# Thirteen products without a reader taken out between the router and the first gate product of a decoder block

## What is computed

```python
x = x + mix @ w_o[l]
h = rms_norm(x, norm_ffn_g[l]).reshape(b * s, d)
# moe_ffn, cut:
logits = (h @ w_router + b_router).astype(jnp.float32)
top_val, top_idx = lax.top_k(logits, TOP_K)
gates = jax.nn.softmax(top_val, axis=-1).astype(h.dtype)
# for every expert e, on the tokens that chose it:
g = xb @ w_gate[e] + b_gate[e]
u = xb @ w_up[e] + b_up[e]
g = jnp.minimum(g, SWIGLU_LIMIT)
u = jnp.clip(u, -SWIGLU_LIMIT, SWIGLU_LIMIT)
glu = g * jax.nn.sigmoid(SWIGLU_ALPHA * g)
out = ((u + 1.0) * glu) @ w_down[e] + b_down[e]
```

## Time and profile before

| | |
|---|---|
| median of 3 runs | 1124.85 us (1124.01 to 1125.22) |
| the profiled execution, its own time | 1124.24 us |
| its span in the trace | 1122.5 us, so 1.7 us lie around it |
| PE busy | 1066.8 us (95%) |
| DVE, ACT, POOL busy | 222.9, 126.1, 20.0 us |
| DMA traffic | 438.16 MB, 390 GB/s over the span |
| mean granted PE clock over the span | 0.988 of full speed |

### The profile page before, as it was taken

How to read it: one execution, slowest core, us unless ns; L and a number is a source line. 1 busy time by engine, 2 the same in 40 slices (tenths; PEclk the granted TensorE clock), 3 DMA queues, 4 the chain that set the end, 5 groups by cost and what they waited for, 6 DMA issues and landing times.

```text
span 1122.5 us, 11859 instructions
## 1 busy us (share of the span) xinstructions
PE 1066.8 (95%) x5057; PEld 504.1 (45%) x5057; DVE 222.9 (20%) x507; ACT 126.1 (11%) x226; POOL 20.0 (2%) x21
## 2 busy tenths in 40 slices
PE   9999999999999999999999898989898989999886
PEld 8888887634343443344334332433243324343322
DVE  5442223321112030203112110020203020202021
ACT  1201340210010001000100010000000100010002
POOL 2300000000000000000000000000000000000000
PEclk9999999999999999999999999999999999999999
DMA  8975256599999999999999999999999999999995
GB/s 339 391 307 225 85 216 281 197 403 429 434 431 431 429 431 430 433 430 433 432 433 431 430 433 431 433 430 433 433 432 431 430 433 431 433 426 426 429 427 241
DMA packets 26654, 438.16 MB, mean 390 GB/s; under 512 B 4992, under 2 KB 6272, under 8 KB 8576
## 3 DMA queue, kind: packets, MB, share of 16 engines
q1 hardware_dynamic: 26480, 437.67, 92.1%
q10 hardware_dynamic: 144, 0.07, 0.0%
HBM read 436.28 MB, written 1.05 MB: 390 GB/s over the span
## 4 chain that ended last, share of the span: by engine, by line
PE 58%; DMA 40%; ACT 1%; issue 0%; DVE 0%; another core or an unknown queue 0%; SPq 0%; ACTq 0%; DVEq 0%
DMA ring<-in_experts 40%; PE ps L1593 24%; PE ps L1639 9%; PE ps L1226 9%; PE ps L1402 2%; PE ps L1241 2%; PE ps L1507 2%; PE ps L1648 2%; PE ps L1276 1%; PE ps L1450 1%; PE ps L1447 1%; PE ps L1628 1%; PE ps L1516 1%; ACT region_va L708 0%; PE ps L1526 0%; DMA ring<-in_first 0%
## 5 line engine op out<-in xcount | busy, mean ns | idle before, releaser
L1593 PE MATMUL ps<-ring,xT 128*64 128x512 f32 x2048 | 462.8, 607 | 24.1 <-DMA ring<-in_experts 24.1
L1593 PEld LDWEIGHTS ps<-ring,xT 128*64 128x64 f32 x2048 | 145.0, 139 | 315.8 <-issue 283.6
L1639 PE MATMUL ps<-ring,region_va 128*64 128x512 f32 x1024 | 228.3, 596 | 22.9 <-ACT region_va L708 12.3
L1639 PEld LDWEIGHTS ps<-ring,region_va 128*64 128x64 f32 x1024 | 73.3, 137 | 156.4 <-issue 125.8
L1226 PE MATMUL ps<-ring 128*128 128x256 f32 x448 | 98.7, 380 | 0.0
L1226 PEld LDWEIGHTS ps<-ring 128*128 128x128 f32 x448 | 84.5, 190 | 11.8 <-issue 0.2
L1125 DVE TENSOR_SCALAR g<-ps 128x1024 f32<-128x1024 f32 x16 | 19.6, 1224 | 348.5 <-PE ps L1593 348.5
L1507 PEld LDWEIGHTS ps<-sel,x 128*128 128x128 f32 x480 | 55.4, 192 | 9.5 <-issue 9.5
L1648 PE MATMUL ps<-g,g_T 128*128 128x512 f32 x128 | 59.2, 605 | 0.0
L1147 DVE TENSOR_SCALAR region_va<-ps 128x512 f32<-128x512 f32 x32 | 22.1, 691 | 184.4 <-PE ps L1593 184.4
L1072 DVE TENSOR_TENSOR xT<-ps,g_ffn 128x512 f32<-128x512 f32 x30 | 20.7, 691 | 190.9 <-PE ps L1507 190.9
(11 more groups left out here) (218 smaller groups left out, 476.8 us busy)
## 6 DMA issues: line engine op xcount, KB each, us to landing
ring<-in_experts SPq DMA_DIRECT2D x71, 4096.0 KB, 46.2
ring<-in_experts SPq DMA_DIRECT2D x43, 2048.0 KB, 46.2
ring<-in_head SPq DMA_DIRECT2D x13, 2048.0 KB, 13.3
ring<-in_experts SPq DMA_DIRECT2D x14, 1024.0 KB, 8.5
ring<-in_first SPq DMA_DIRECT2D x7, 384.0 KB, 6.4
x<-in_x SPq DMA_DIRECT2D x2, 512.0 KB, 24.0
out<-x SPq DMA_DIRECT2D x4, 256.0 KB, 2.3
ring<-in_norm_final_g SPq DMA_DIRECT2D x1, 512.0 KB, 11.5
```

Source lines behind the costliest of these rows:

```text
L1593: last = mm(bank(banks + half)[rows, :], xT[:, 2 * m + c, rows], w[:, c, k, half * W512:(half + 1) * W512], start=False, stop=m == 3 and c ...
L1639: last = mm(bank(first + half)[rows, :], hTm[:, 2 * m + c, rows], w[:, c, k, half * W512:(half + 1) * W512], start=m == 0 and c == 0, stop ...
```

## The change

The helper `fill` and its four calls are deleted, thirteen products in all: two behind the w_o products, two behind the last transposes, seven behind the last logits, two behind the gate biases. All waits stay, and so does every other instruction of every engine. Where the fills stood, PE's next instruction is now its next wait.

```diff
             last.then_inc(wo_done, 1)
 
-            def fill(n):
-
-                for _ in range(n):
-                    mm(bank(6), su_b[0:3 * E, :], bias3[0:3 * E, 0, 0:W512], start=True, stop=True)
-
             pe.wait_ge(ld_bias3, 16 * 12)
-            fill(2)
             router_transposes_quarter(1)
-            fill(2)
             pe.wait_ge(hTr_dve, 3)
             router_logits(1, range(6, KC))
-            fill(7)
 
             r = bank(4)
             pe.wait_ge(mask_ready, 2)
@@
             pe.wait_ge(oh_ready, 1)
             biases(0, 0, pair_bank(0))
-            fill(2)
```

## The result

The changed kernel takes 1126.74 us (median of 20 runs, 1126.05 to 1128.38), the kernel before in the same set of runs 1124.47 us (20 runs, 1123.99 to 1125.44). The ratio is 1.0022, with a 95% interval from 1.0015 to 1.0028: 2.3 us slower. The shortest of the 20 runs is longer than the longest of the kernel before, so the difference is real, and it lies on the 0.2% (2.25 us) up to which the prediction counted a time as the same. The profiled execution took 1126.70 us, its span is 1124.8 us. Lines behind the deleted ones have moved up: the counts stand in lines 1490 to 1493, the biases in 1508, the gathering in 1517, the gate and up products in 1584, the down products in 1630.

What follows compares the result with a forecast made beforehand. Bound: the stream of expert weights, whose start hangs on the first gate product. Low stretch 1.1 us less 0.06 gives 1.04, about 1.0 after the queue; 1124.85 + 1.0 = 1125.8 us, range 1124.4 to 1127.2.

Steps and rivals of the forecast that it cites:

- the same: Whole kernel: a time within 0.2% (2.25 us) of the kernel before; chance 0.90, against slower 0.07 and faster 0.03.
- The fall of the clock: Router stage: PE, idle 2.3 us in three pieces, drops to half clock once, for 3.4 us.
- the price of the low stretch: Gathering and perhaps first gate instructions: half clock from about 222.3 to 225.7 us costs 1.1 us.
- my lower bound: Low stretch falling mostly into the waits, from 220.7 to 224.1 us, covering 0.8 us of the gathering: costs 0.4 us.
- The upper bound: One low stretch wholly under work of the path: costs 1.7 us.
- The gain of 0.06 us: Between mask and weight load for the counts: removing the seven fills frees 0.06 us, bounds 0 and 0.12.
- Passing on the delay: From the issue at 227.28 us, 1.04 us late, onward: stream, every rung and the end come about 1.0 us later.
- The clock stays up: Rival, router stage: no single pause is long enough to lower the clock; 1124.8 us, chance 0.12.
- The low stretch doesn't stay alone: Rival, gathering and first gate product: a second low stretch follows; 1128.1 us, or 1126.8 if cheaper; chance 0.09.
- the cheaper of the two forms: Two low stretches, the first mostly in the pauses: 2.0 us late, 1126.8 us.
- The delay is hidden anyway: Rival, queue at the gate product: old pieces last longer, so nothing moves despite a low stretch; 1124.8 us, chance 0.08.
- Theory B: Rival stated with the experiments: about a microsecond of the 2.3 us comes from something besides the clock; no chance given.

Runs made afterwards that it cites:

- e6: Kernel before with only the three pairs of fills taken out, the group of seven kept: 1125.23 us against 1124.50, ratio 1.0006.
- e11: Kernel before, unchanged, in a second profiled execution: 1124.33 us.
- e1: The changed kernel once more, with a further profiled execution: 1126.67 us against 1124.79 of the kernel before, ratio 1.0017.
- e9: The changed kernel once more, a further profiled execution: 1126.69 us in that execution.
- e5: Kernel before with ten more fill products behind the gate biases (fill(12) for fill(2)): 1126.60 us against 1124.50, ratio 1.0017.
- e2: Kernel before with five more fill products behind the gate biases (fill(7) for fill(2)): 1125.23 us against 1124.79, ratio 1.0005.
- e3: Kernel before with only the group of seven fills taken out, the three pairs kept: 1126.29 us against 1124.79, ratio 1.0014.
- e4: Kernel before with all thirteen fill products kept but cut from 512 to 16 columns each: 1126.68 us against 1124.79, ratio 1.0018.

## Why the prediction was right, and by how much it was off

**The bound and the verdict were right.** The stream of weights sets the end, its start hangs on the first gate product with next to no cover, and the time moved by 0.2%, to the bound between "the same" and "slower". Forecast was 1125.8 us with a range to 1127.2; measured 1126.74. The forecast chance of "the same" was too high, though: the measured +2.27 us lies on the bound of 2.25 us, and the interval of the ratio reaches to both sides of it.

**The fall of the clock was right, but the argument for it isn't shown.** In six of six traces it fell, with no pause above 1.45 us, and in e6 behind none above 0.61 us. The Trainium skill, page "TensorE: Matmul & The Clock Gate", section "Why this matters for your kernels", warns only of longer single gaps; where it and these runs differ, the runs decide. My argument was that the pauses add up, 2.3 us as in the one wait of rows 7 that was followed by a fall. The sum doesn't decide either. In e6 two pauses of 0.61 + 0.52 = 1.13 us were enough. And a single wait of 2.25 to 2.28 us in the ladder is followed by a fall in some executions and not in others: in the first trace of the kernel before the product behind it took 8.6 to 8.8 us all seven times, in e11, the same kernel, four times of seven, and in the six traces of the changed kernel 10 times of 34; each other time it took 7.09 us, full clock. So that it fell in six of six here is measured, and which property of the stage brings it about is open. In part the forecast was lucky: by the row of a single fall it could as well have gone the other way.

**The term that was mis-sized is the price of the low stretch.** I put its start at 222.3 us, 3.7 us behind the addition, just above the middle of the bounds 0.4 and 1.7 us. The single low stretches of the six executions begin 3.6 to 5.0 us behind it, so they lie under the gathering more than I took them to, and cost 1.14 to 1.66 us. The one that began early, at 2.6 us, didn't give the cheap 0.4 us of my lower bound. It went on for 6.8 us and cost the most. So the case behind my lower bound wasn't seen in the changed kernel at all. Mean of the six: 1.56 us where I had 1.04. The upper bound was sound: in e1, where the whole stretch lies under work, it cost 1.66 us. The row of 3.79 us from the start of the kernel, by which I priced the gathering, doesn't show what I took it for, since the granted clock is recorded as 1.00 there; but the gathering of e9, wholly at half clock, took 3.78 us.

**The gain of 0.06 us isn't there.** In the changed kernel the mask is ready at 222.26 + 0.18 = 222.44 us, and the weight load for the counts starts 0.11 us behind it, where rows 5 had 0.12:

```profile
222.55 0.10 PEld L1490 LDWEIGHTS ps<-region_va,one_b 128*128 128x128 bf16 x1 [1.53 <-issue]
```

So the seven products held up nothing. The hand-over to the transposes even grew, from 219.12 - 219.06 = 0.06 us (the addition of rows 6 takes 0.42 us in DVE's timeline) to 219.58 - 219.43 = 0.15 us.

**Passing on the delay was right at the end, not on the way.** e5 shows with the clock out of play that it isn't hidden. I had said that every rung would stand later by as much as the issue, and in the table at e11 the rungs stand later by 0.2 to 1.0 us less than the issue. What lies between the mean delay of 1.56 us and the 2.07 us of the same six executions isn't settled. The distance from issue to end is on average 0.5 us longer than in the two traces of the kernel before, also in the two kernels that never lose the clock here (898.0 us in e2, 897.4 us in e5). So it isn't the clock in this stage; whether it belongs to a stream that starts late, or to two executions of the kernel before that happened to be short ones (its medians were 1124.47 to 1124.79 us), stays open. So does the rest up to the 2.27 us of the medians.

**The rivals.** "The clock stays up" didn't happen in the changed kernel, but e3, where some executions keep the old time, is compatible with it for less idle time; those executions have no profile. "The low stretch doesn't stay alone" happened in one execution of six, in the cheaper of the two forms I had worked out: 2.26 us of delay, where I had 2.0, and not 3.4, since a part of it lay in the pauses. "The delay is hidden anyway" fell with e5. Theory B fell as to the layout of the program, with e4; half a microsecond of it is left at most.

## What to carry to other kernels

Work without a reader can be worth keeping where it stands in waits just ahead of work on the critical path: it cost nothing here, and taking it out cost 2.3 us. When pauses are judged for what they do to the clock, neither the longest nor their sum told here what would happen: 1.13 us in two pieces were followed by a fall, and single waits of 2.25 us often weren't. Trace several executions, and expect the loss to change from one to the next. Filler in some of the waits only can do harm: in e6 it ran at half clock, took 2.88 us in place of 1.68 and stood in front of the real work.

## What the runs showed of the hardware beyond that

The low stretches of PE's clock in the router stage lasted 3.4 us, or 6.8 us in e9. They began in a pause (e9) or up to 0.8 us after the last one (e6: logits from 220.24, low from 221.02 us). The hand-over from DVE to the transposes took 0.15 us in the changed kernel, where PE had waited 0.61 us, and 0.06 us where fills had kept it busy until shortly before. Waiting alone doesn't explain it: in e4, behind a wait of 0.48 us, it took 0.06 us as well (addition over at 218.95, transposes at 219.01 us).
